# Attentions: the pair outputs move ahead of VectorE's next copy, the turn of the attention output goes tile by tile, and ScalarE copies the odd heads' turned probabilities in the differential attention

## What is computed

```
p = softmax(q k^T + mask)                       # every head
hybrid:        o[head] = p v                     -> tok, 16 heads x 64
differential:  o[pair] = p1 v - lam * (p2 v)     # even head, odd head
               o = rms_norm(o[pair]) * subln     -> tok, 8 pairs x 128
h = h + tok @ w_out
```

## Time and profile before

| | |
|---|---|
| median of 3 runs | 1394.65 us (1394.26 to 1394.74) |
| the profiled execution | 1396.2 us, span 1394.2 us |
| TensorE busy | 1286.8 us, 92% |
| VectorE, ScalarE, GpSimd busy | 662.3, 548.2, 36.7 us |
| mean granted TensorE clock | 0.976 |
| hybrid attention (first to last pair output) | 97.2 to 118.1 us |
| differential attention | 419.4 to 448.7 us |
| latent attentions | about 737 to 760 and 1089 to 1116 us |

### The profile page before, as it was taken

One profiled execution on the slowest core, in us unless ns is written; L12 is line 12 of the kernel. 1 busy time (PEld: TensorE's weight loads), 2 busy tenths in 40 slices (PEclk: granted clock), 3 DMA queues, 4 the chain that ended last, 5 costly groups with the idle time before them and its releaser, 6 DMA issues.

```text
span 1394.2 us, 19006 instructions
## 1 busy us (share of the span) xinstructions
PE 1286.8 (92%) x7252; PEld 932.3 (67%) x7252; DVE 662.3 (48%) x1321; ACT 548.2 (39%) x1072; POOL 36.7 (3%) x75
## 2 busy tenths in 40 slices
PE   7999899999996899999899789999879987999986
PEld 5878899997875799999777544344357874443432
DVE  6656666666757566666666621111056463110102
ACT  5455544445445554444656311111044641111101
POOL 0000000000003000000200000000000000000000
PEclk9999999999999999999999999999999898999999
DMA  9532455554550265555432969999974096999995
GB/s 344 182 121 91 139 190 184 181 181 151 181 181 1 92 210 182 186 187 185 139 122 105 378 256 423 420 420 421 422 264 153 23 387 228 416 422 421 421 421 232
DMA packets 68570, 336.80 MB, mean 242 GB/s; under 512 B 7888, under 2 KB 8016, under 8 KB 47376
## 3 DMA queue, kind: packets, MB, share of 16 engines
q1 hardware_dynamic: 68400, 335.50, 64.2%
q0 software_dynamic: 96, 0.30, 0.1%
HBM read 334.72 MB, written 1.05 MB: 241 GB/s over the span
## 4 chain that ended last, share of the span: by engine, by line
PE 76%; DVE 7%; DMA 7%; ACT 5%; issue 2%; POOL 1%; SPq 1%; DVEq 0%; ACTq 0%; POOLq 0%
PE bank L1358 15%; PE bank L1360 15%; PE bank L1359 15%; PE bank L1649 13%; DMA expert_part<-stream 7%; PE bank L1676 6%; PE bank L1606 2%; DVE w_low L815 2%; PE bank L1495 1%; ACT tok L497 1%; PE bank L1689 1%; ACT w_high L487 1%; ACT probs L533 1%; PE bank L1434 1%; PE bank L1410 1%
## 5 line engine op out<-in xcount | busy, mean ns | idle before, releaser
L815 DVE TENSOR_TENSOR w_low<-raw,w_high 128x1024 fp32r<-128x1024 f32 (+1 forms) x246 | 285.5, 1211 | 131.3 <-ACT w_high L487 131.0
L487 ACT ACTIVATE w_high<-raw 128x1024 fp32r<-128x1024 f32 (+1 forms) x246 | 241.6, 1042 | 43.6 <-PE bank L1360 43.2
L1649 PE MATMUL bank<-expert_part,slots_x 128*64 128x512 f32 x1024 | 233.0, 593 | 9.3 <-DMA expert_part<-stream 8.1
L1358 PE MATMUL bank<-x_high,w_high 128*128 128x256 f32 (+1 forms) x712 | 203.2, 285 | 3.8 <-DVE x_low L834 3.5
L1359 PE MATMUL bank<-x_low,w_high 128*128 128x256 f32 (+1 forms) x712 | 202.7, 285 | 0.0
L1360 PE MATMUL bank<-x_high,w_low 128*128 128x256 f32 (+1 forms) x712 | 202.7, 285 | 0.0
L1649 PEld LDWEIGHTS bank<-expert_part,slots_x 128*64 128x64 f32 x1024 | 76.8, 137 | 159.0 <-issue 138.2
L1358 PE MATMUL bank<-w_high,x_high 128*128 128x512 f32 (+1 forms) x416 | 163.3, 393 | 5.1 <-DVE x_low L834 3.2
L1359 PE MATMUL bank<-w_low,x_high 128*128 128x512 f32 (+1 forms) x416 | 161.2, 387 | 0.0
L1360 PE MATMUL bank<-w_high,x_low 128*128 128x512 f32 (+1 forms) x416 | 160.9, 387 | 0.0
L1125 DVE SCALAR_TENSOR_TENSOR expert_hid<-expert_gate,combine,bank 128x256 f32<-128x256 f32 x32 | 15.4, 481 | 304.8 <-ACT expert_gate L640 304.8
(11 more groups left out here) (249 smaller groups left out, 1572.2 us busy)
## 6 DMA issues: line engine op xcount, KB each, us to landing
expert_part<-stream SPq DMA_DIRECT2D x164, 1024.0 KB, 17.9
raw<-stream SPq DMA_DIRECT2D x244, 512.0 KB, 5.2
expert_part<-stream SPq DMA_DIRECT2D x56, 512.0 KB, 17.8
const_sb<-const SPq DMA_DIRECT2D x1, 2070.0 KB, 13.4
residual<-x SPq DMA_DIRECT2D x2, 512.0 KB, 4.1
final_gain<-fgain SPq DMA_DIRECT2D x2, 512.0 KB, 8.8
out<-residual SPq DMA_DIRECT2D x2, 512.0 KB, 2.9
small_sb<-small SPq DMA_DIRECT2D x1, 765.0 KB, 5.9
```

Source lines behind the costliest of these rows:

```text
L487: nc.scalar.activation(wh[:, u, cols], raw[:, u, cols], ACT.Copy).then_inc(w_high, 1)
L815: tt(wl[:, u, cols], raw[:, u, cols], wh[:, u, cols].bitcast(F32), ALU.subtract).then_inc(w_low, 1)
L1358: mm(o, ah, bh, start=start, stop=False, **kw)
L1649: ins = mm(B[0][half * CAP:(half + 1) * CAP, :], xg[p // 4 % 2][:, k, x_of], w[k % 4 // 2][:, k % 2 * 512:(k % 2 + 1) * 512], start=k == 0 ...
```

## The change

1. In all four attentions VectorE's order becomes `scores(a+2)`, `outputs(a)`, `probs(a+1)`. The reciprocal is taken once for a pair, at its odd head.
2. In the differential attention ScalarE copies the turned probabilities of the odd heads (`odd_turned`), each right after the exponentials of the next even head. The factor lambda goes into the sum (`scalar_tensor_tensor` in place of `tensor_tensor`), and the small operation L888 is gone.
3. In the first two attentions the output is turned tile by tile: 14 transposes of the tiles 0 to 6 in two steps, each of which waits only for its own heads, and the two of tile 7 (`last_tile`) in the middle of the out projection, after its first chunk. The banks are 4, 6, 7 and 2. In the differential attention ScalarE splits tiles 0 and 1 ahead of the last pair's squares, and VectorE splits tiles 0 to 4 ahead of the last pair's scaling.

```diff
@@ -146,3 +146,4 @@
 T_BASE = [sum(T_TILES[:q]) for q in range(len(T_TILES) + 1)]
-T_BANKS = [2 * (n // 3) for n in T_TILES]
+T_BY_TILE = (1, 4)
+T_BANKS = [5 if q in T_BY_TILE else 2 * (n // 3) for q, n in enumerate(T_TILES)]
 T_BANK_BASE = [sum(T_BANKS[:q]) for q in range(len(T_BANKS) + 1)]
@@ -153,2 +154,10 @@
     return 2 * (k // 4) + k % 2, k % 4 // 2
+def t_bank(q, b):
+    return (4, 6, 7, 2)[b] if q in T_BY_TILE else 4 + b
+def t_event(q, k):
+    return T_BANK_BASE[q] + (5 if q in T_BY_TILE and k == 7 else t_place(k)[0] + 1)
@@ -499,11 +509,11 @@
-            def high(q, dst, gain, free):
+            def high(q, dst, gain, free, tiles=None):
                 act.wait_ge(chunk_used, free) if free else None
-                for k in range(T_TILES[q]):
+                for k in range(T_TILES[q]) if tiles is None else tiles:
                     b, at = t_place(k)
-                    act.wait_ge(t_done, T_BANK_BASE[q] + b + 1)
+                    act.wait_ge(t_done, t_event(q, k))
                     if at:
                         act.wait_ge(t_low, T_BASE[q] + k - 1)
-                    nc.scalar.activation(dst[:, k, :], B[4 + b][:, at * S:at * S + S], ACT.Copy, scale=gain(k)).then_inc(t_high, 1)
+                    nc.scalar.activation(dst[:, k, :], B[t_bank(q, b)][:, at * S:at * S + S], ACT.Copy, scale=gain(k)).then_inc(t_high, 1)
@@ -538,2 +548,9 @@
                         between(a)
+            def odd_turned(a):
+                act.wait_ge(p_tr, 16 + a + 1)
+                if a >= 2:
+                    act.wait_ge(pv_done, 16 + a - 1)
+                nc.scalar.activation(prT[:, 1, :], B[7][:, 0:384], ACT.Copy).then_inc(odd_pT_ready, 1)
@@ -705,5 +722,13 @@
             projections(C_DIFF, 4, 16)
-            softmaxes(16, range(2, 16), head_squares)
+            def beside_l1(a):
+                if a % 2 == 0:
+                    odd_turned(a - 1)
+                head_squares(a)
+            softmaxes(16, range(2, 16), beside_l1)
+            odd_turned(15)
+            high(T_L1O, xh, lambda k: gain_sub[:, 0:1], C_DIFF_OUT, range(2))
             head_squares(17)
-            high(T_L1O, xh, lambda k: gain_sub[:, 0:1], C_DIFF_OUT)
+            high(T_L1O, xh, lambda k: gain_sub[:, 0:1], 0, range(2, 8))
             plain(C_DIFF_OUT, 3)
@@ -829,7 +854,7 @@
-            def low(q, dst, hi, gain):
-                for k in range(T_TILES[q]):
+            def low(q, dst, hi, gain, tiles=None):
+                for k in range(T_TILES[q]) if tiles is None else tiles:
                     b, at = t_place(k)
                     dve.wait_ge(t_high, T_BASE[q] + k + 1)
-                    stt(dst[:, k, :], B[4 + b][:, at * S:at * S + S], gain(k), hi[:, k, :].bitcast(F32),
+                    stt(dst[:, k, :], B[t_bank(q, b)][:, at * S:at * S + S], gain(k), hi[:, k, :].bitcast(F32),
                         ALU.mult, ALU.subtract).then_inc(t_low, 1)
@@ -878,4 +903,8 @@
                     dve.wait_ge(p_tr, first + a + 1)
-                    step[0] += 1
-                    nc.vector.reciprocal(rden[:, a, :], den[:, a, :]).then_inc(dve_step, 1)
+                    if a % 2:
+                        step[0] += 1
+                        nc.vector.reciprocal(rden[:, a - 1:a + 1, :], den[:, a - 1:a + 1, :]).then_inc(dve_step, 1)
+                        scale_step[a] = step[0]
+                    if diff and a % 2:
+                        return
                     if a >= 2:
@@ -883,8 +912,2 @@
                     nc.vector.tensor_copy(prT[:, a % 2, :], B[turned_bank + a % 2][:, 0:384]).then_inc(pT_ready, 1)
-                    if diff and a % 2:
-                        dve.wait_ge(dve_step, step[0])
-                        step[0] += 1
-                        ts(rden[:, a, :], rden[:, a, :], lamb[:, 6:7], None, ALU.mult).then_inc(dve_step, 1)
-                    scale_step[a] = step[0]
@@ -907,3 +930,4 @@
                     dve.wait_ge(dve_step, step[0])
-                    tt(tok[:, :, a // 2 * dv:(a // 2 + 1) * dv], both[:, 0], both[:, 1], ALU.add).then_inc(o_done, 2)
+                    stt(tok[:, :, a // 2 * dv:(a // 2 + 1) * dv], both[:, 1], lamb[:, 6:7], both[:, 0], ALU.mult, ALU.add)\
+                        .then_inc(o_done, 2)
@@ -920,5 +944,5 @@
                             scores(a + 2)
+                        outputs(a)
                         if a + 1 < n:
                             probs(a + 1)
-                        outputs(a)
                         if between is not None:
@@ -1243,4 +1267,5 @@
             rest()
+            low(T_L1O, xl, xh, lambda k: gain_sub[:, 0:1], range(5))
             last_head_norm()
-            low(T_L1O, xl, xh, lambda k: gain_sub[:, 0:1])
+            low(T_L1O, xl, xh, lambda k: gain_sub[:, 0:1], range(5, 8))
             out_projection(C_DIFF_OUT)
@@ -1422,2 +1447,21 @@
                     ins.then_inc(t_done, 1)
+            def tile_transposes(q, done, counts):
+                for b in range(4):
+                    if b % 2 == 0:
+                        pe.wait_ge(done, counts[b // 2])
+                    for k in (k for k in range(7) if t_place(k)[0] == b):
+                        for t in range(NT):
+                            at = t_place(k)[1] * S + t * P
+                            ins = nc.tensor.transpose(B[t_bank(q, b)][:, at:at + P], tok[:, t, k * P:(k + 1) * P], ident)
+                    ins.then_inc(t_done, 1)
+            def last_tile(q, done, count):
+                pe.wait_ge(done, count)
+                pe.wait_ge(t_low, T_BASE[q] + 6)
+                for t in range(NT):
+                    ins = nc.tensor.transpose(B[t_bank(q, 3)][:, S + t * P:S + (t + 1) * P], tok[:, t, 7 * P:8 * P], ident)
+                ins.then_inc(t_done, 1)
@@ -1489,2 +1533,10 @@
+                def turned_ready(a):
+                    if diff and a % 2:
+                        pe.wait_ge(odd_pT_ready, a // 2 + 1)
+                    elif diff:
+                        pe.wait_ge(pT_ready, first + a // 2 + 1)
+                    else:
+                        pe.wait_ge(pT_ready, first - (8 if first > 16 else 0) + a + 1)
                 def turn(a):
@@ -1492,3 +1544,3 @@
                     if a >= 2:
-                        pe.wait_ge(pT_ready, first + a - 1)
+                        turned_ready(a - 2)
                     for j in range(3):
@@ -1498,3 +1550,3 @@
                 def values(a):
-                    pe.wait_ge(pT_ready, first + a + 1)
+                    turned_ready(a)
                     if a >= 4 and a % 2 == 0:
@@ -1533,6 +1585,8 @@
-            def out_projection(c0, q):
+            def out_projection(c0, q, last=None, count=None):
                 for half in range(2):
-                    run(group(c0 + 2 * half, 2, [B[2 * half][:, :], B[2 * half + 1][:, :]], 512, None if half else q,
-                              bank_done))
+                    for j in group(c0 + 2 * half, 2, [B[2 * half][:, :], B[2 * half + 1][:, :]], 512, None if half else q,
+                                   bank_done):
+                        if last is not None and half == 0 and j == 0:
+                            last_tile(q, last, count)
@@ -1788,4 +1842,5 @@
             pe.wait_ge(const_in, 16)
-            transposes(T_L0O, tok, tokens_ready())
-            out_projection(C_HYB_OUT, T_L0O)
+            tokens_ready()
+            tile_transposes(T_L0O, o_done, (8, 14))
+            out_projection(C_HYB_OUT, T_L0O, o_done, 16)
             normed_transposes(T_F0)
@@ -1799,4 +1854,5 @@
             rest()
-            transposes(T_L1O, tok, tokens_ready())
-            out_projection(C_DIFF_OUT, T_L1O)
+            tokens_ready()
+            tile_transposes(T_L1O, head_normed, (4, 7))
+            out_projection(C_DIFF_OUT, T_L1O, tok_ready, toks[0])
             normed_transposes(T_F1)
```

More of the change, by code:

```diff
@@ L301, in build @@
         zero_ready = sem("zero_ready")
+        odd_pT_ready = sem("odd_probsT_ready")
         head_normed = sem("heads_normed")
```

## The result

The changed kernel takes 1401.88 us (median of 6 runs, 1400.69 to 1405.97), the kernel before beside it 1394.70; the ratio is 1.0051 [1.0041, 1.0062]. So it is slower by 7 us, and outside the range of the prediction.

A forecast was written before the change was run, and what follows sets the result against it. Hybrid attention bound by TensorE's work and an equal 3.06 us round through three engines, differential by a 4.21 us round. 3.15 - 0.45 + 2.26 - 5.50 + 1.0 = +0.46 us, so 1395.1 us; range 1391.2 to 1398.8.

The forecast's parts named there:

- clock 1.00 throughout: Differential attention: sign expected if right, with a period of 4.4 to 4.5 and L906 to first product about 2 us.
- rivals of 0.15, 0.14 and 0.13: Differential tail clock falls, 1397.5 us (0.15); second latent half-clock stretch vanishes, 1391.9 (0.14), or appears in the first too, 1398.3 to 1399 (0.13).
- The slower rival: Differential tail: the clock falls all the same, slowing transposes and first products, +2.4 us, 1397.5; chance 0.15.
- The rival: Second latent attention's half-clock stretch, 3.2 us lost: vanishes, 1391.9 (0.14), or appears in the first too, 1398.3 to 1399 (0.13).
- The rounds: Hybrid round 3.06 to 3.51 us, +3.15 over seven intervals; differential round +0.27, six of them +1.62.
- lambda, put at nothing: Differential rounds: the factor lambda in the sum costs nothing, since L888 was off the round.
- Last pair of the differential attention: Differential attention, last pair: 2.85 us becomes 3.49, +0.64, as the copy of head 15 waits for the squares of pair 6.
- The copy of 384 columns on ScalarE: Differential rounds: odd copy taken as 0.53 us, between 0.47 and 0.59; with handover, +0.16 a round (bounds +0.10 and +0.22).
- The tails: Ends of two attentions: hybrid -0.45 us (-0.69 and +0.24 for late transposes), differential -5.50, first product 2.10 after L906.
- The first latent attention: Latent attentions: +0.3 at heads 3 and 4, some +0.2 at one more place; both attentions +1.0 (0 to 1.4).
- the prediction's own sign of being wrong: Whole kernel: wrong if hybrid period stays 3.06, second tile step waits for GpSimd's scaling, or the clock differs in an untouched stage.

The follow-up runs named there:

- Filled waits: Changed kernel with unused transposes of the identity filling TensorE's waits in the hybrid attention: 1400.04 us, ratio 1.0026 to the kernel before.
- the one trace without a fall: Changed kernel with VectorE's old order in the two latent attentions only: 1399.40 us, ratio 1.0024 to the kernel before.
- the tiles alone: Changed kernel with VectorE's old order everywhere and VectorE copying all heads; tile-by-tile turn, pair reciprocal and lambda in the sum kept: 1391.12 us, ratio 0.9971.
- the delay: Kernel before with three unused VectorE copies of 768 columns, each waited for, ahead of the second latent attention's norm: 1393.22 us, ratio 0.9971.
- the first and third experiment: Changed kernel with the old order everywhere: first with VectorE copying all heads, 1391.12 us; third with ScalarE's odd copies kept, 1390.58 us.
- one lengthens it: Changed kernel with the old order everywhere and one unused VectorE copy ahead of the second latent attention's norm: 1392.36 us, ratio 0.9966.
- the changed kernel with three copies: Changed kernel, new order kept, with three unused VectorE copies of 768 columns ahead of the second latent attention's norm: 1396.46 us, ratio 1.0004.
- the three idle copies: Changed kernel with the old order everywhere and three unused VectorE copies of 768 columns ahead of the second latent attention's norm: 1388.70 us, ratio 0.9941.
- the second four experiments: Old order in latent attentions only, 1399.40 us; kernel before with new order there, 1399.11, or three unused copies, 1393.22; old order in differential attention only, 1400.27.

## Why the prediction was wrong

**The step that failed is the clock.** The prediction added changed rounds and tails at the clock of the trace before, with "clock 1.00 throughout" in the differential attention and the latent stretch at its old length, and put the clock's answers into rivals of 0.15, 0.14 and 0.13. The lengthened rounds came as worked out, within 0.02 us a round and 0.12 in the hybrid attention's last pair; the clock is nearly the whole miss. It fell in three places:

- *Hybrid, last pair.* The prediction had no term and no rival here. Filled waits show the cause, as far as one trace can: the clock fell in the traces of all five kernels with the new order and unfilled waits (at 116.2 to 122.0, for 3.4 to 10.2 us), in none of the eight with the old order before 143 us, and not with the waits filled. Cost in the changed kernel: 146.75 against 145.45, 1.3 us; in the others up to 3.6. A spell in the feed-forward behind it, which seven of the nine kernels without the fall have from 144 to 148 us on, takes part of this back: the changed kernel has none there.
- *Differential, last rounds.* The slower rival said 2.4 us for a clock that falls there all the same. It fell, a little ahead of the place where the rival had it, and cost 137.39 - 135.39 = 2.0 us against the one trace without a fall. The stage came out at -0.79 where -3.24 was forecast, and this fall is 2.0 of the 2.45 between them. The argument against it, that waits of 0.98 us in the rounds had left the clock at 1.00, was read from rounds with scores in them; the last ones have none. The new order isn't needed for this fall: it is there with the old one as well (at 443.9 with the tiles alone, 444.3 with ScalarE's copies), once the hole is gone. That thin work is the cause here too was not tried by filling, and one trace of the same code, as thin, had no fall. So its cause stays open.
- *Second latent attention.* The rival let the stretch vanish or appear in the first one as well. What it did was to double, for 3.3 us. The order goes with the length in all ten traces without the delay: 10.2 us in the four kernels with the old order, the kernel before among them, and 20.5 in the six with the new. How the order does it is not shown, since TensorE has no gap in the first 10.2 us of either. What comes ahead of the norm decides whether there is a stretch. The prediction also read it short: its window began at 1108, the stretch at 1104.1, so that 3.2 us of lost clock stood for 5.1.

**The rounds.** Hybrid 3.53 us for a forecast 3.51. Differential 4.50 for 4.48, by errors that nearly cancel: the order cost 0.15 instead of 0.11, the odd copy 0.09 instead of 0.16, and lambda, put at nothing, 0.06. The sum with lambda in it (0.48 us for the 0.43 of the plain sum) is on the round's path after all: the squares wait for it. Last pair of the differential attention at full clock 3.51 for 3.49; that of the hybrid one 2.63, for 2.06 + 0.45 = 2.51.

**The copy of 384 columns on ScalarE** took 0.47 us; I had 0.53, in the middle of the earlier trace rows. The Trainium skill (VectorE: DVE Perf Modes, the section on the TRN2 errata) gives 172 cycles and one for each element at 1.2 GHz; an estimate by it for 384 columns is 0.46 us, and the trace agrees. For the 256 columns of the earlier trace rows the same estimate is 0.36 us where the trace has 0.47, so the agreement is with this copy alone. The middle of the two rows was no safe guide: 384 columns took as long as those 256.

**The tails.** Hybrid -0.18 with the late transposes for a forecast -0.45 (from last output to norm 25.06 us, before 25.24), since the transposes ran at half clock in part; at full clock, in the filled kernel, it is 24.47 us, -0.77. Differential: from last output to norm 24.88 us instead of 30.21, -5.33 for -5.50. This gain is real and is what the first and third experiment keep.

**The first latent attention** +0.77 for +0.5, the second +0.5 at full clock, together +1.3 for a forecast +1.0 (0 to 1.4).

**Where the rest comes from.** The -1.39 in the untouched feed-forward is a spell at half clock that stood at 148.4 to 151.8 before and is missing in the changed kernel's trace: the prediction's own sign of being wrong, a clock that differs in a stage the change doesn't touch. Of the +5.80 in the span, sizes of rounds and tails account for about 1.0 (filled hybrid +2.5, differential -2.8, latent +0.8 and +0.5); the clock's answers for 1.3 + 2.0 + 3.3 - 1.4 = 5.2; -0.4 is what the other untouched stages show. The Trainium skill (TensorE: Matmul & The Clock Gate, Part 1) says that the slow clock is the default and that activity releases it. The filled waits agree in the hybrid attention. That the second latent attention falls to half with TensorE busy, stays there through 10.2 us without a gap, and keeps the fast clock after a longer rest ahead, is no case of that rule.

**What stays open.** Why three copies ahead of the norm remove the stretch and one lengthens it to 17.1 us. The runs do not separate the longer rest from the later place: three copies bring both, 10.2 instead of 6.8 us at half around the norm and 1.9 us of shift. That the changed kernel with three copies, 5.5 us later at this attention's first output than the kernel before with them (1105.50 and 1099.98), and the old order, 5.3 us earlier (1094.72), both run their heads at full clock speaks for the rest and against a place. Open too are why the new order keeps the clock down for longer, and what makes it fall in the last differential rounds.

**A version that beats both** is the old order with tiles and ScalarE's odd copies: 0.9954 [0.9939, 0.9970] as it is, 0.9941 [0.9927, 0.9955] with the three idle copies; the intervals overlap, so both are shown to be gains over the kernel before, and the copies' step over the first is not.

## What to carry to other kernels

Before a loop is lengthened, look at the waits that it gives the bounding engine, above all in the last rounds, where part of its work has run out: in the hybrid attention TensorE, busy 2.70 of 4 us instead of all of it, lost its fast clock, which cost 1.3 us on top of the 2.5 that the stage grew without the fall. The busy share alone does not tell, though: in the differential attention 3.83 of 6 us went at 1.00. A queue behind a wait is free only if what the wait delays isn't first in the next round; so take the period link by link, as here, but price the clock as a term of its own, with a measured spell at either end of the range. When a stage is compared between two kernels, read its granted clock first: here three useless copies made a kernel faster, with more clock. And trace several kernels with the same code in a stage before a spell is put down to the code.

## What the runs showed that was not expected

- Three useless copies, 1.9 us of delay, shortened the next attention by 3.6 us in the kernel before and in the old order, and by 7.2 in the changed kernel (115.41 to 108.18 us).
- Useless transposes in TensorE's waits kept the clock at 1.00 in the hybrid attention and shortened the stage by 1.3 us; in the same trace the clock fell behind the norm instead.
- The same instructions up to 116 us, in four kernels, had spells at half of 3.4, 6.8, 10.2 and 10.2 us behind them. Runs of one kernel lie apart by as much: the changed kernel's six by 5.3 us, the kernel before's six by 2.9 and, beside the second four experiments, its 28 by 5.5.
- The second latent attention ran at 0.50 for 10.2 to 20.5 us with TensorE busy nearly all the time, while the first one, with the same code, had at most 3.4 us of it.
